# FFN loop: gate product in two wide halves between down products, and seven block products by chained weight sums

## The reference

```python
def swiglu(x, w_gate, w_up, w_down):
    return (jax.nn.silu(x @ w_gate) * (x @ w_up)) @ w_down
...
    for l in range(DEPTH):
        x = layer_norm(ALPHA * x + FFN_RESIDUAL * swiglu(x, ffn1_w_gate[l], ffn1_w_up[l], ffn1_w_down[l]),
                       ln1_g[l], ln1_b[l])
...
        x = layer_norm(ALPHA * x + FFN_RESIDUAL * swiglu(x, ffn2_w_gate[l], ffn2_w_up[l], ffn2_w_down[l]),
                       ln3_g[l], ln3_b[l])
```

## Time and profile before

| | us |
|---|---|
| median of 3 runs | 965.9 (965.71 to 966.23) |
| the profiled execution | 965.6 |
| its span, first to last instruction | 963.9 |
| TensorE busy | 954.2 (99%) |
| TensorE weight loads busy | 852.6 (88%) |
| VectorE busy | 840.1 (87%) |
| ScalarE busy | 600.3 (62%) |

### The profile page before, as it was taken

One profiled execution on the slowest core, in us unless ns is written; L12 is line 12 of the kernel. 1 busy time (PEld: TensorE's weight loads), 2 busy tenths in 40 slices (PEclk: granted clock), 3 DMA queues, 4 the chain that ended last, 5 costly groups with the idle time before them and its releaser, 6 DMA issues.

```text
span 963.9 us, 16417 instructions
## 1 busy us (share of the span) xinstructions
PE 954.2 (99%) x6058; PEld 852.6 (88%) x6058; DVE 840.1 (87%) x1033; ACT 600.3 (62%) x703; POOL 21.2 (2%) x53
## 2 busy tenths in 40 slices
PE   9999999999999999999999999999999999999996
PEld 9998989899788989898899898998987889989895
DVE  7999998855899999998899999978568999999985
ACT  6655665568884756565566665655688756656553
POOL 0000000001000000000000010000010000000000
PEclk9999999999999999999999999999999999999999
DMA  8577645572344656454635584554542445646454
GB/s 321 203 261 257 233 165 187 205 262 88 132 168 143 223 189 234 167 224 178 219 131 203 189 305 174 218 177 174 218 149 109 166 159 205 228 165 227 167 185 161
DMA packets 34650, 187.25 MB, mean 194 GB/s; under 512 B 3888, under 2 KB 3888, under 8 KB 19504
## 3 DMA queue, kind: packets, MB, share of 16 engines
q1 hardware_dynamic: 33120, 177.22, 50.6%
q0 software_dynamic: 1488, 9.45, 2.6%
HBM read 185.61 MB, written 1.05 MB: 194 GB/s over the span
## 4 chain that ended last, share of the span: by engine, by line
PE 96%; DVE 2%; ACT 0%; DMA 0%; issue 0%; DVEq 0%
PE bank L1500 29%; PE bank L1356 22%; PE bank L1357 22%; PE bank L1358 22%; PE bank L1419 1%; DVE xn L950 1%; PE bank L1698 1%; DVE xn L969 1%; DVE qT L984 0%; DMA qT<-first 0%; ACT scratch L528 0%; DVE w_lo L916 0%; PE bank L1714 0%; DVE lt L999 0%; PE bank L1569 0%
## 5 line engine op out<-in xcount | busy, mean ns | idle before, releaser
L1356 PE MATMUL bank<-xT,w_hi 128*128 128x256 f32 x944 | 267.6, 283 | 0.0
L1358 PE MATMUL bank<-xT,w_lo 128*128 128x256 f32 x944 | 267.1, 283 | 0.0
L1357 PE MATMUL bank<-xT,w_hi 128*128 128x256 f32 x944 | 267.1, 283 | 0.0
L483 ACT ACTIVATE w_hi<-raw 128x2048 fp32r<-128x2048 f32 x116 | 221.5, 1909 | 1.4 <-DMA raw<-stream 1.4
L1500 PE MATMUL bank<-xT,w_hi 128*128 128x512 f32 (+1 forms) x608 | 184.8, 377 | 0.4 <-ACT w_hi L843 0.4
L1356 PEld LDWEIGHTS bank<-xT,w_hi 128*128 128x128 f32 x944 | 181.0, 192 | 2.6 <-issue 0.7
L1357 PEld LDWEIGHTS bank<-xT,w_hi 128*128 128x128 f32 x944 | 181.0, 192 | 1.7
L1358 PEld LDWEIGHTS bank<-xT,w_lo 128*128 128x128 f32 x944 | 181.0, 192 | 0.0
L858 DVE TENSOR_TENSOR w_lo<-raw,w_hi 128x2048 fp32r<-128x2048 f32 x54 | 123.5, 2287 | 21.6 <-ACT w_hi L483 21.4
L1500 PEld LDWEIGHTS bank<-xT,w_lo 128*128 128x128 f32 x560 | 102.9, 188 | 22.1
L1356 PE MATMUL bank<-w_hi,h_hi 128*128 128x512 f32 x284 | 111.4, 392 | 0.0
(11 more groups left out here) (173 smaller groups left out, 1491.8 us busy)
## 6 DMA issues: line engine op xcount, KB each, us to landing
raw<-stream SPq DMA_DIRECT2D x110, 1024.0 KB, 4.9
raw<-stream SPq DMA_DIRECT2D x110, 512.0 KB, 4.5
lnp<-ln_gb POOLq DMA_DIRECT2D x6, 1024.0 KB, 5.3
band<-rel_band POOLq DMA_DIRECT2D x2, 1024.0 KB, 9.4
xn<-x POOLq DMA_DIRECT2D x1, 1024.0 KB, 7.5
out<-xn SPq DMA_DIRECT2D x4, 256.0 KB, 2.1
qT<-first SPq DMA_DIRECT2D x2, 384.0 KB, 4.0
kT<-first SPq DMA_DIRECT2D x2, 384.0 KB, 5.0
```

Source lines behind the costliest of these rows:

```text
L483: nc.scalar.activation(w_hi[:, at(slot if into is None else into)], raw[:, slot, :], ACT.Copy).then_inc(hi_ready, 1)
L1356: nc.tensor.matmul(o, w[0], x[0], start=start, stop=False, skip_group_check=again)
L1357: nc.tensor.matmul(o, w[0], x[1], start=False, stop=False, skip_group_check=again)
L1358: return nc.tensor.matmul(o, w[1], x[0], start=False, stop=stop, skip_group_check=again)
```

## The change

The gate of the steps j = 2 to 8 takes the form of the up halves: two halves of 16 matmuls, each into bank[0], each copied out by ACT into `gate_sums`; DVE adds the two sums of both halves (`gate_sum`), and ACT takes the silu of the result (`silu_sums`). TensorE's order in a step becomes: first gate half; the rest of the step before (two matmuls of product 6, and product 4); second gate half; products 2 and 1; first up half; product 3 and two matmuls of product 5; second up half; the last matmul of product 5, product 7 and the first of product 6. The wait for the second gate copy is the line ahead of `step(j, stop)`.

The seven block products are chosen anew (Winograd's form): three blocks of the weights are used as they are, and four sums are formed, the last two each from the one before it. The h sums form a chain of four, too. The order of ACT's, DVE's and SP's queues follows. `gather` adds partial sums first and then puts them into `xn`.

The core of the diff (left out: renamed counters, slices of the parts, the first steps of an FFN):

```diff
-STRASSEN = {1: (5, 6), 2: (2, 1), 3: (6, 3), 4: (0, 2), 5: (1, 0), 6: (4, 5), 7: (3, 4)}
+WINOGRAD = {1: (0, 0), 2: (6, 2), 3: (4, 1), 4: (5, 6), 5: (1, 3), 6: (2, 5), 7: (3, 4)}
...
@@ SP: loads of a loop @@
-                with sp.Fori(1, SF) as j:
-                    load(2, first + 3 * j + 5)
-                    sp.wait_ge(lo_part, 2 * strassen(l, f, j) + 1)
-                    sp.wait_ge(wsum_done, 3 * strassen(l, f, j) + 3)
-                    fetch(1, first + 3 * j + 7)
+                with sp.Fori(1, SF - 1) as j:
                     load(0, first + 3 * j + 6)
+                    load(2, first + 3 * j + 8)
+                    sp.wait_ge(lo_part, 2 * seven_step(l, f, j + 1) + 1)
+                    sp.wait_ge(wsum_done, 3 * seven_step(l, f, j + 1) + 3)
+                    fetch(1, first + 3 * j + 10)
...
@@ ACT @@
+                def copy_gate(j, c):
+
+                    act.wait_ge(*((unit_used, used(l, base + 3 * j + 2)) if c else
+                                  (gate_first, wide_gate(l, f, j) + 1)))
+                    nc.scalar.activation(gate_sums[:, c, :], bank[0][:, :], ACT.Copy).then_inc(gate_copied, 1)
+
+                def silu_sums(j):
                     act.wait_ge(hf_done, it(l, f, j) + 1)
-                    silu(j + 1, 3 * j + 2)
+                    act.wait_ge(gate_summed, wide_gate(l, f, j) + 1)
+                    nc.scalar.activation(sg.rearrange("p (c t) -> p c t", c=2), gate_sums[:, :, 0:T],
+                                         ACT.Silu).then_inc(silu_done, 1)
...
+                def last_of_h_and_parts(j):
+                    act.wait_ge(unit_used, used(l, base + 3 * j + 1))
+                    high_h(j)
+                    split_last_parts_hi(l, f, j)
+
+                def step(j, more=True):
+                    up_hi(j + 1)
+                    differences(j)
+                    copy_gate(j, 0)
+                    last_of_h_and_parts(j)
+                    copy_gate(j, 1)
+                    next_gate(j)
+                    silu_sums(j)
+                    copy_up(j + 1, 0)
+                    if more:
+                        next_pure(j + 1)
+                    copy_up(j + 1, 1)
...
@@ DVE @@
+            def weight_chain(l, f, j):
+                n = 3 * seven_step(l, f, j)
+                dve.wait_ge(wsum_done, n + 1)
+                nc.vector.tensor_tensor(wsum[:, 1024:1536], raw[:, 1, 1024:1536], wsum[:, 0:512],
+                                        ALU.subtract).then_inc(wsum_done, 1)
+                dve.wait_ge(wsum_done, n + 2)
+                nc.vector.tensor_tensor(wsum[:, 1536:2048], raw[:, 1, 1536:2048], wsum[:, 1024:1536],
+                                        ALU.subtract).then_inc(wsum_done, 1)
...
+                def gate_sum(j):
+
+                    dve.wait_ge(gate_copied, 2 * wide_gate(l, f, j) + 2)
+                    nc.vector.tensor_tensor(gate_sums[:, :, 0:T], gate_sums[:, :, 0:T], gate_sums[:, :, T:2 * T],
+                                            ALU.add).then_inc(gate_summed, 1)
+
+                def low_parts(j):
+                    split_up_lo(l, base + 3 * j + 3, 0)
+                    split_differences_lo(l, f, j)
+                    split_up_lo(l, base + 3 * j + 3, 1)
+                    low_h(j)
                     split_last_parts_lo(l, base + 3 * j + 4)
+                    gate_sum(j)
+
+                def next_unit(j):
                     weight_sums(l, f, j + 1, FILLED[base + 1] + 2 + j)
-                    split_pure_lo(l, f, j + 1)
                     split_lo(l, base + 3 * j + 5, 2)
                     up_sum(j + 1, 0)
-                    split_differences_lo(l, f, j + 1)
+                    split_pure_lo(l, f, j + 1)
                     up_sum(j + 1, 1)
                     h_sums(j + 1)
...
@@ TensorE @@
+                def gate_half(j, c):
+
+                    if c == 0:
+                        pe.wait_ge(lo_ready, split(l, base + 3 * j + 2))
+                        pe.wait_ge(up_copied, 2 * wide(l, f, j) + 2)
+                    else:
+                        pe.wait_ge(gate_copied, 2 * wide_gate(l, f, j) + 1)
+                    wide_half(2, c).then_inc(unit_used if c else gate_first, 1)
+
+                def up_half(j, c):
+
+                    if c == 0:
+                        pe.wait_ge(up_lo_first, (2 * l + f) * (SF - 1) + j)
...
-                def step(j, start=False, stop=False):
-                    n = strassen(l, f, j)
+                def rest(stop=False):
+
+                    product(6, signal=m_done if stop else None, parts=(1, 2))
+                    product(4, signal=unit_used)
+
+                def step(j, stop=False):
+                    n = seven_step(l, f, j)
                     finished = m_done if stop else None
-                    gate(j)
                     pe.wait_ge(hlo_done, it(l, f, j) + 1)
                     pe.wait_ge(lo_part, 2 * n + 1)
-                    product(5, start, finished)
-                    product(2, start, m_done if stop else pure_used)
+                    product(2)
+                    product(1, signal=finished)
                     up_half(j, 0)
+                    product(3, signal=None if stop else pure_used)
                     pe.wait_ge(lo_part, 2 * n + 2)
-                    product(4, start, finished)
-                    product(3, start, m_done if stop else parts_used)
+                    product(5, parts=(0, 1))
                     up_half(j, 1)
+                    product(5, signal=finished, parts=(2,))
+                    product(7, signal=m_done if stop else parts_used)
                     pe.wait_ge(lo_ready, split(l, base + 3 * j + 4))
-                    product(1, start, finished)
-                    product(6, start)
-                    product(7, start, unit_used)
+                    product(6, parts=(0,))
+
+                def step_with_gate(j, stop=False):
+                    gate_half(j, 0)
+                    rest()
+                    gate_half(j, 1)
+                    pe.wait_ge(gate_copied, 2 * wide_gate(l, f, j) + 2)
+                    step(j, stop)
...
-                with pe.Fori(1, SF - 1) as j:
-                    step(j)
-                step(SF - 1, stop=True)
+                gate(1)
+                pe.wait_ge(silu_done, it(l, f, 1) + 2)
+                step(1)
+                with pe.Fori(2, SF - 1) as j:
+                    step_with_gate(j)
+                step_with_gate(SF - 1, stop=True)
+                rest(stop=True)
```

More of the change, by code:

```diff
@@ L197, in trunk @@
         Y = [[bank[4], bank[5]], [bank[6], bank[7]]]
[L198 to L199 removed]
+        M = {k: bank[b] for k, b in ((1, 1), (2, 2), (3, 3), (4, 7), (5, 5), (6, 6), (7, 4))}
+        FFN_Y = [[M[5], M[4]], [M[3], M[2]]]
         Z = [bank[2], bank[3], bank[4], bank[5], bank[2], bank[3]]
@@ L639, in ffn, with next_pure @@
-                act.sem_inc(up_copied, 2)
-                next_unit(0, gate=False)
-                with act.Fori(1, SF - 1) as j:
-                    step(j)
[L643 to L647, removed]
+                def next_pure(j):
+                    act.wait_ge(raw_ready[1], loaded(l, 1, first[1] + 1 + j))
+                    act.wait_ge(pure_used, (2 * l + f) * (SF - 1) + j)
+                    split_pure_hi()
@@ L648, in ffn @@
+                act.sem_inc(up_copied, 2)
+                next_pure(1)
+                differences(1)
+                up_hi(2)
+                last_of_h_and_parts(1)
+                act.wait_ge(hf_done, it(l, f, 1) + 1)
+                silu(2, 5)
+                next_gate(1)
+                copy_up(2, 0)
+                next_pure(2)
+                copy_up(2, 1)
+                with act.Fori(2, SF - 1) as j:
+                    step(j)
+                step(SF - 1, more=False)
                 split_hi(l, base + 3 * SF + 3, 0, first[0] + 1 + SF)
@@ L1012, in layer_norm, with gather, add @@
                     x_lo(phase(l, p + 1), (2, 3))
-            def gather(l, f, half_of):
+            def gather(l, f, part):
                 n = 2 * l + f
-                def add(count, tb, half, m, op, first=False, after=0):
+                both, three = wsum[:, 0:512], wsum[:, 512:1024]
+                def add(tb, half, block, first=False, after=0):
                     cols = slice(512 * half, 512 * half + 512)
-                    dve.wait_ge(m_done, n * 5 + count)
                     if after:
@@ L1530, in up_half @@
                             last = plain(bank[0][:, :], w_hi[:, w], xT[:, :, kc, :], stop=kc == KC - 1)
-                    last.then_inc(unit_used if c else up_first, 1)
-                def product(m, start, signal=None):
-                    a, b = STRASSEN[m]
-                    w = at(1, seven(b))
-                    last = three(M[m][:, :], (h_hi[:, a, :], h_lo[:, a, :]), (w_hi[:, w], w_lo[:, w]), start,
-                                 signal is m_done, True)
+                    return last
@@ L1538, in product @@
```

(8 more changed lines are left out.)

173 lines of the change are left out of this document (89 added, 84 removed).

## The result

The changed kernel is slower: 996.28 us median (996.02 to 996.78) against 965.82 for the kernel before, a ratio of 1.0314 [1.0303, 1.0325]. The forecast was 991.5 us, in a range of 986 to 998. Sign, mechanism and range hold; about 5 us of the loss were not in the sum. The profiled execution took 996.1 us, of which the span is 994.4: 30.5 more than before.

A forecast was written before the change was run, and what follows sets the result against it. The prediction took TensorE, busy 99% of the span, as the bound. Its sum was 965.6 - 5.0 (gate's matmuls) + 26.9 (second gate copy waits) + 3.8 (silu waits at j = 1) = 991.3 us; it forecast 991.5, range 986 to 998.

The forecast's parts named there:

- The price of one wait: Behind the second gate half: ACT start 0.43, copy 0.60, release to weight load 0.05, slower matmul 0.11; loss 0.96 us a step, 26.9 in all.
- 1.0 with a few hundredths of latency more: Upper bound, in us, of one TensorE wait for the second gate copy; the lower bound was 0.85, the value taken 0.96.
- the 986 to 996: Interval of the kernel's time, in us, given as the prediction's own forecast, with chance 0.82.
- The upper end of 997.7: Slow bound of the kernel's time in us: 32 waits x 1.0 - 1.1 + 1.2 for the FFN ends = 32.1 us more.
- The wait at j = 1: Narrow gate's silu wait, now ahead of step: 0.32 until ACT starts, 0.96 us each, 3.8 us over four FFNs.
- The gate's matmuls: Steps j = 2 to 8: 48 matmuls (5.75 us) become two halves (5.57 us); gain 0.18 us a step, 5.0 in all.
- The covered copies: The three other bank[0] copies by ACT: 1.08 us to release against 1.36 until needed, margin 0.28; no cost.
- The stall itself is VectorE's cover: VectorE's added sums need some 0.5 us more a step; TensorE's wait hides this, without it spare falls from 1 us to 0.3.
- the walk: One looped step timed from the gate's first half: low_h ends at about 6.3, TensorE returns at 7.66; no second wait.
- The hidden copy: Rival: TensorE gets past the second gate copy's wait or runs products 2 and 1 ahead of it; 960.6 us, chance 0.06.
- The second wait behind VectorE: Rival: VectorE's chain of sums makes low_h end after TensorE's return; at 0.4 us a step 11.2 us, 1002.5, chance 0.08.
- the wide gate saves nothing: Rival: a gate half costs more beside other products than an up half does; 996.3 us, chance 0.04.

## Why the prediction was right, and what it mis-sized

- **Where the loss comes from: right.** The wait for the second gate copy stops products 2 and 1, and one full trip from TensorE to ACT and back is paid in every gated step; the same at j = 1. Shown from both sides: moved behind the products the loss is gone, and put alone into the kernel before it makes the loss.
- **The price of one wait: right in three of four parts, one mis-sized.** Start of ACT 0.44 (said 0.43), copy 0.60 (0.60), slower products behind it 0.13 (0.11). The step that failed is "from a releaser's end to TensorE's next weight load 0.05", taken from the earlier trace rows. It holds where the matmul itself holds the late wait, as in the four last steps; in the 24 looped ones the wait stands two places ahead of the matmul and it is 0.21. This term and the few hundredths beside it: 24 x 1.18 + 4 x 1.0 = 32.3 against the 26.9 of the sum. The bound of "1.0 with a few hundredths of latency more" was too tight by the same 0.18.
- **That the range held is in part luck.** The median lies 0.3 above the 986 to 996 that got the chance of 0.82. The upper end of 997.7 left 3.9 us of room because it counts the gate's gain at 1.1 us instead of 5.0. The gain came in full, and that room took up the latency that the bound of 1.0 lacked; with the sum's own 5.0 the upper end would have been 993.8.
- **The wait at j = 1: right,** 4.0 against 3.8 (ACT started 0.38 after the last matmul and not 0.32).
- **The gate's matmuls: right, a little too small,** 5.9 against 5.0: the products behind a wide half are 0.03 us faster a step too. That gave back part of the missing latency.
- **The covered copies, VectorE, loads, ends of an FFN at nothing: right for this kernel.** TensorE waits for nothing else in the loop. VectorE is busy for 15.41 of 17.08 (said 15.6 of 16.89). The 15.97 of the earlier trace rows was misread: it is not overlaps of neighbours, since in the step of the earlier trace rows the same view counts 15.05 us, which is 16.11 less the wait of 1.04. In the step of the earlier trace rows, the one from j = 3 on, VectorE was still catching up; so the trace of before showed already that it enters the loop late. The kernel before, the steps from j = 2 and from j = 5 on (columns as in the earlier trace rows):

```profile
55.42:71.65 16.23, 16.23 (x103) 14.66 (x102) 16.09 (x19) 9.83 (x10) 0.87 (x1) 1.00 0.74 277
...
103.88:119.99 16.11, 16.11 (x104) 14.55 (x102) 15.05 (x18) 9.75 (x9) 0.00 (x0) 1.00 0.56 197
```

  The moved sums of `gather` fell into VectorE's idle time before the last down unit, as said: in order of time,

```profile
173.74 1.89 DVE L1067 SCALAR_TENSOR_TENSOR xn<-xn,stick_t 128x512 f32<-128x512 f32 x3
...
178.44 2.29 DVE L897 TENSOR_TENSOR w_lo<-raw,w_hi 128x2048 fp32r<-128x2048 f32 x1 [0.61 <-ACT w_hi L497]
```

  0.61 us of waiting for ACT are left of the 2.08 of the earlier trace rows.
- **"The stall itself is VectorE's cover, and without it the spare would shrink from 1 us to 0.3": right in kind.** Without the stall the steady loop keeps up, with 15.33 us busy in 15.90; at the entry of the loop it doesn't, which the walk through one steady step could not show. The holes there are worth 3.4 us.
- **The rivals.** The hidden copy: TensorE came back 0.86 us late and never ran products 2 and 1 ahead of the wait. The second wait behind VectorE: low_h was done 0.67 us before TensorE's return in the step shown and 1.5 in the later ones of that loop (the walk had 1.36); it appears only where the stall is taken out. That the wide gate saves nothing would have given 996.3, the measured time to a tenth, and is wrong all the same: its saving was measured at 0.23 us a step. The time alone would have pointed to the wrong rival.

## What to carry to other kernels

A wait belongs ahead of the instruction that needs the data, not at the end of the stage that makes it: whatever stands between, on an engine that works in order, was the cover. Where several waits stand together, the one that comes last in time should be held by the instruction that does the work: here that was the last one in the code in the looped steps and the first in those with constants, so look at the program's queue and not at the code alone. And when a stall is removed, look at once at the engines that were late behind it, at the entry of the loop above all: here 3.7 of 5.9 us were lost there again.

## What the runs showed of the hardware

- From a release to TensorE's next weight load it takes 0.05 us if the matmul's own wait is the late one, and 0.12 or 0.21 if the late wait stands one or two places ahead on register instructions, about 0.09 for each place, in loops with waits against registers. With constant waits two of the three stand on one semaphore instruction, and the late one costs 0.05 more as the second there and 0.09 as the first (1.08, 1.13 and 1.18 us from start to start).
- The next weights are not loaded ahead of a wait: in every stall shown the load itself starts only after the release (57.25, 74.70, 73.78), and in the traces it is the load that holds the matmul's wait. By the Trainium skill's weight loads that are pulled ahead ("TensorE: Matmul & The Clock Gate", the table at its head) a stall would cost about 0.1 us less, the prediction's estimate; past a wait the trace shows none of that.
- Two matmuls of 256 columns cost about 0.013 us more than one of 512 with the same columns (2 x 0.120 - 0.227); 16 fewer starts in a step save 0.23 us with what follows.
